# TensorE's order within a round of the state space layer, rearranged

## The reference, cut to what matters

```python
u = (h @ w_in).reshape(bsz, t, S5_GROUPS, S5_GROUP)      # 64 groups of 16 channels
bu = einsum('btgi,gpi->btgp', u, bb)                     # complex, 64 states a group
x = associative_scan(combine, (ab, bu), axis=1)          # x_t = ab * x_(t-1) + bu_t
y = einsum('gip,btgp->btgi', c_re, x_re) - einsum('gip,btgp->btgi', c_im, x_im) + d_skip * u
za, zg = split(gelu(y) @ w_glu, 2);  return za * sigmoid(zg)
...
mod = (silu(c) @ w_ada[layer] + b_ada[layer])            # six vectors of 1024 a layer
```

## Time and profile before

| | us |
|---|---|
| median of 3 runs (1852.01 to 1853.23) | 1852.79 |
| the profiled execution's own time | 1851.18 |
| its span, first to last instruction | 1849.4 |

### The profile page before, as it was taken

How to read it: one execution, slowest core, us unless ns; L and a number is a source line. 1 busy time by engine, 2 the same in 40 slices (tenths; PEclk the granted TensorE clock), 3 DMA queues, 4 the chain that set the end, 5 groups by cost and what they waited for, 6 DMA issues and landing times.

```text
span 1849.4 us, 27100 instructions
## 1 busy us (share of the span) xinstructions
PE 1719.4 (93%) x9191; PEld 1448.7 (78%) x9191; DVE 1385.1 (75%) x1560; ACT 1206.3 (65%) x1504; POOL 179.5 (10%) x202
## 2 busy tenths in 40 slices
PE   6988899997499877999999999999999999999995
PEld 3867699986387775888888888888888888888884
DVE  3564445460855454899999999999999999999997
ACT  3623455301275354688888888888888888878885
POOL 1041000000735300520000000000000000000001
PEclk8988999999688588999999999999999999999997
DMA  9662644434134336799999999999999999999995
GB/s 364 253 254 98 241 173 160 181 153 168 73 138 158 133 143 273 289 421 382 404 375 367 398 361 397 378 364 403 365 391 383 354 406 376 380 386 360 396 373 201
DMA packets 72292, 549.01 MB, mean 297 GB/s; under 512 B 8192, under 2 KB 8463, under 8 KB 15264
## 3 DMA queue, kind: packets, MB, share of 16 engines
q1 hardware_dynamic: 69186, 538.54, 74.5%
q0 software_dynamic: 2496, 8.35, 1.3%
q10 hardware_dynamic: 542, 1.20, 0.2%
HBM read 528.65 MB, written 19.44 MB: 296 GB/s over the span
## 4 chain that ended last, share of the span: by engine, by line
PE 87%; DVE 5%; ACT 4%; DMA 2%; issue 1%; ACTq 0%; POOL 0%; DVEq 0%; SPq 0%
PE bank L1907 85%; PE bank L2356 1%; DVE parts L1351 1%; DMA arena<-in_state_conv_dram 1%; DMA ring<-in_dense_rows_dram 1%; DVE w_lo L462 1%; ACT w_hi L456 1%; DVE rstd L1344 1%; ACT arena L1177 1%; PE bank L2335 0%; PE bank L2211 0%; DVE sq L1515 0%; DMA fT<-y_rows,row_i 0%; DVE sq L1362 0%; ACT plain_hi L1102 0%
## 5 line engine op out<-in xcount | busy, mean ns | idle before, releaser
L1907 PE MATMUL bank<-w_hi,parts 128*128 128x512 f32 x3024 | 897.9, 392 | 1.5 <-DVE parts L1829 1.5
L509 DVE TENSOR_TENSOR w_lo<-ring,w_hi 128x1024 fp32r<-128x1024 f32 x654 | 785.4, 1223 | 56.9 <-ACT w_hi L504 18.7
L504 ACT ACTIVATE w_hi<-ring 128x1024 fp32r<-128x1024 f32 x654 | 690.5, 1061 | 154.7 <-PE bank L1907 154.6
L1907 PEld LDWEIGHTS bank<-w_hi,parts 128*128 128x128 f32 x3024 | 563.1, 188 | 115.8 <-issue 1.7
L1907 PE MATMUL bank<-w_lo,parts 128*128 128x512 f32 x1512 | 548.8, 390 | 0.0
L1907 PE MATMUL bank<-parts,w_hi 128*128 128x264 f32 x1600 | 312.9, 297 | 50.8 <-DVE parts L1351 36.2
L1907 PEld LDWEIGHTS bank<-w_lo,parts 128*128 128x128 f32 x1512 | 283.9, 188 | 59.8
L1907 PEld LDWEIGHTS bank<-parts,w_hi 128*128 128x128 f32 x1600 | 261.2, 199 | 63.4 <-issue 21.9
L462 DVE TENSOR_TENSOR w_lo<-ring,w_hi 128x2048 fp32r<-128x2048 f32 x50 | 114.8, 2299 | 187.9 <-ACT w_hi L456 187.8
L1907 PE MATMUL bank<-parts,w_lo 128*128 128x264 f32 x800 | 234.4, 293 | 0.0
L1907 PEld LDWEIGHTS bank<-parts,w_lo 128*128 128x128 f32 x800 | 158.3, 198 | 0.0
(11 more groups left out here) (407 smaller groups left out, 1357.5 us busy)
## 6 DMA issues: line engine op xcount, KB each, us to landing
ring<-in_expert_rows_dram SPq DMA_DIRECT2D x330, 1024.0 KB, 5.8
ring<-in_dense_rows_dram SPq DMA_DIRECT2D x48, 2048.0 KB, 8.1
hT<-in_expert_rows_dram SPq DMA_DIRECT2D x55, 1024.0 KB, 5.8
ring<-in_dense_rows_dram SPq DMA_DIRECT2D x8, 1408.0 KB, 6.2
x_rows<-arena SPq DMA_DIRECT2D x1, 7168.0 KB, 19.5
y_rows<-arena SPq DMA_DIRECT2D x10, 512.0 KB, 6.5
arena<-x_rows SPq DMA_DIRECT2D x9, 512.0 KB, 6.9
ring<-in_dense_rows_dram SPq DMA_DIRECT2D x2, 1024.0 KB, 4.8
```

Of the source, the lines that this page charges most:

```text
L504: act.activation(hi_slots[u % AHEAD], raw_unit(u), ACT.Copy).then_inc(hi_ready, 1)
L509: dve.tensor_tensor(lo_slots[u % AHEAD], raw_unit(u), hi_slots[u % AHEAD].bitcast(F32), ALU.subtract).then_inc(lo_ready, 1)
L1907: return pe.matmul(out, lhsT, rhs, start=start, stop=stop, skip_group_check=True)
```

## The change

`matrices(k)` is cut into two functions, `turns_of_b(k)` and `lag_products(k)`, each with the waits that its part had. The order within a round becomes: turns of block k+1, modulation's piece 16+k, outputs of block k-2, lag products of block k+1, sums of block k+1, rows of piece 15+k. Before it was: turns, lag products, outputs, sums, piece, rows. No instruction is added or taken away; the other engines' streams are the same.

```diff
-            def matrices(k):
+            def turns_of_b(k):
...
                 ins.then_inc(tr_full, 1)
+
+            def lag_products(k):
+
                 if k:
                     pe.wait_ge(k_pad_ready, k)
...
-            matrices(0)
+            turns_of_b(0)
+            lag_products(0)
             chunk_sums(0)
             for k in range(KT + 2):
                 if k + 1 < KT:
-                    matrices(k + 1)
+                    turns_of_b(k + 1)
+                if k < KT:
+                    ada(16 + k)
                 if k >= 2:
                     outputs(k - 2)
                 if k + 1 < KT:
+                    lag_products(k + 1)
                     chunk_sums(k + 1)
-                if k < KT:
-                    ada(16 + k)
                 if 1 <= k <= KT:
                     ada_rows(15 + k)
```

## The result

The changed kernel takes 1859.72 us (median of seven runs, 1853.08 to 1861.61) against 1852.01 for the kernel before (seven runs beside it, 1844.3 to 1853.82): a ratio of 1.005, interval 1.0031 to 1.0069. The forecast was 1858.9.

A forecast was written before the change was run, and what follows sets the result against it. TensorE was taken to bound the state space stage, at half clock for more than half of it. The stage's +6.1 us on the profiled 1851.18 gave 1857.3, plus 1.6 for the median 1858.9; range 1842 to 1865.

The forecast's parts named there:

- The wait at piece 17: Start of the stage: TensorE stands still until ACT empties bank 0 of modulation's piece 16, 4.2 us.
- Rounds 1 and 2: Behind piece 17: half clock until piece 18, a rise in it, turns of block 4 starting at 570.2.
- A full round: Mid-stage rounds: a clock fall behind the lag products and a rise at the piece in each, 12.9 us.
- The tail's wait: Before the outputs of block 6: POOL pads and rotates 4.2 us behind block 5's outputs, plus 0.2 hand-over.
- The sum: State space stage, from its start to its last outputs: 6.1 us longer than before.
- any difference outside the stage: Sign of being wrong: any part of the time difference lying outside the state space stage.
- DVE's chain: Lags, scan and rotation after the later lag products: between nothing and 0.3 us a round, taken as nothing.
- Rival 1: Full rounds: the clock holds, no fall behind the lag products; about -13 us, 1840; chance 0.2.
- Rival 2: Full rounds: rises are missed, such rounds cost 19.1 instead of 12.9; +18 to +25, some 1875; chance 0.08.
- The transposes: Turns beside the piece: by the skill's rule they would not help the clock rise; given little weight.

The follow-up runs named there:

- second profile: The changed kernel, unchanged, profiled once more (one execution): 1858.13 us; the kernel before, likewise profiled again, took 1853.35.
- lags_alone: The kernel before with only the lag products moved, behind the outputs: 1865.7 us, ratio 1.0084.

## Why the prediction was right, point by point

- *The wait at piece 17*, put at 4.2, was 4.25, released by ACT's evacuation as said. In the second profile it was 2.5, since a fall in the sums of block 1 had made TensorE later.
- *Rounds 1 and 2*: block 4's turns were forecast for 570.2 and came at 574.81. This is the largest miss. Piece 18 started about when it was forecast but went through at half clock (557.56 to 561.13), so outputs, lag products and sums behind it cost 5.2, 3.4 and 3.5. In the second profile the rise came, and block 4's turns stood at 569.3. Piece 18 had no turns right before it but an idle of 1.27.
- *A full round* was put at 12.9 and is 12.9, with the rise in the piece and the fall in the sums or rows.
- *The tail's wait* for POOL was reckoned from 4.2 us of padding and rotation and 0.2 for the hand-over. From the end of the outputs of block 5 (634.10) to the start of those of block 6 (639.88) it took 5.8 instead of 4.4. The hand-over is 0.36, and POOL took 5.16 from the start of the padding to the end of the rotation, where it took 4.17 in the earlier trace rows. There DVE stood idle; here it scanned and rotated beside POOL. The second padding, 1.04 there, is this row:

```profile
635.34 1.42 POOL L768 TENSOR_TENSOR plain_hi<-plain_lo,minus_half_rows 128x512 f32<-128x512 f32 x1
```

  The outputs of block 5 made up for it in that profile: forecast at half clock with 5.17, they found a rise and took 3.1 (631.01 to 634.10). In the second profile they took 5.2, and the wait for POOL was 5.6 from their end.
- *The sum*: 6.1 forecast for the stage; 9.7 in the first pair of profiles, 6.8 in the second (122.7 against 115.9 from the first turn to the end of the last output), 7.7 between the medians. By parts of the stage (difference of the changed kernel to the one before, us):

| part | forecast | first pair | second pair |
|---|---|---|---|
| first turn to the turns of block 4 | +5.6 | +9.8 | +5.0 |
| the four full rounds, to the end of the rows of piece 21 | -3.2 | -2.9 | -2.9 |
| from there to the end of the last output | +3.7 | +2.8 | +4.7 |

  The mechanism is right part by part. That the median came within 0.8 of 1858.9 is in part luck: the seven executions of the kernel before lie near 1844 to 1848 (three) and 1852 to 1854 (four), and the median fell into the second lot, from which the forecast had started. The forecast also called any difference outside the stage a sign of being wrong; 0.8 us of 10.5 lie outside, but the stage of the kernel before starts 1.7 us apart in its own two profiles.
- *DVE's chain* was put at 0 to 0.3 a round at the full clock; where the clock is held it costs 0.17. Its last link is not DVE's rotation, as reckoned, but POOL's.
- *Too heavy in the argument, though it did the sum no harm*: the clock. I let it carry the story, but the kernel before spends 65 us of its stage at half clock too (0.28 x 2 x 116.0) and the changed one 75. The four full rounds, with a fall and a rise in each, take 51.9 us (574.81 to 626.66); before, with two rounds held and two lost, they took 54.8 (564.59 to 619.36). The loss lies in the parts before and behind them, where the new waits are and, in the first profile, the missed rise at piece 18. With the clock the same in both (lag products and rows wider), some 6 us of waits remain.
- *Rival 1*, the clock holds, was disproved by the windows. With wider lag products the clock does hold over the full rounds, and the stage is 10.2 us shorter than in the first profile of the kernel before (105.8 against 116.0), where this rival had 13; by ratio it is only 0.27%, some 5 us, as the kernel before was faster in that group. In this rival's sum, outputs, rows and outputs at half clock are 5.17 + 1.73 + 5.17 = 12.1, not 11; the 628 goes by 12.1. *Rival 2*, missed rises, occurred in one round of the first profile.
- *The transposes*: the Trainium skill, in "TensorE: Matmul & The Clock Gate" (Part 4, PE-mode transpose), has it that transposes do not bring the full clock. The earlier trace rows speak against it: behind an idle of 3.11 us, sixteen transposes filled the time to 1825.31 and other matmuls the 0.8 us from there to the rise at 1826.1. The rounds here do not decide it. In the changed kernel all pieces of full rounds with turns right before them saw a rise (580.6, 590.8, 604.5), and in lags_alone, with sums before and rows behind, two in a row saw none; but later ones there did, as did pieces with sums before them in the kernel before. Outputs behind the piece instead of rows are another difference, and no run took the turns away.

## What to carry to other kernels

Moving a step forward on an engine that is the bound brings its waits forward with it: ask for each semaphore of the moved step when its giver is due, in the first and last rounds above all, where other work no longer covers it. When a fully busy TensorE runs at half clock, look for matmuls with few moving columns. Giving them more columns, where their weight loads took as long anyway (1.87 us for sixteen), cost nearly nothing here and gave 0.6% to 0.9% in the old order, while reordering around them gave a loss. Putting back the old order at the ends doesn't put back the old waits: the seam has its own.

## What the runs showed of the hardware that was not expected

Sixteen MATMUL records of 16 columns take 1.75 us and of 112 columns 1.82 at the full clock, each with its own 128-column weight load. (Modulation's pieces are the exception among this stage's matmuls: their weight loads have the form 128x32.) In the full rounds of the changed order TensorE is busy in either case, without a gap with the narrow ones and but for 0.17 us a round with the wide ones; the clock behind them fell in each round with the narrow ones and not with the wide ones.
